# A delta layer's scan at five k-steps per chunk in every head pair, with later pairs begun sooner

## What is computed

```python
def gated_deltanet(h, w_in, conv_w, a_log, dt_bias, norm_w, w_out):
    proj = h @ w_in
    qkv = silu(causal_depthwise_conv(proj[..., :3 * DN_WIDTH], conv_w)); z = proj[..., 3 * DN_WIDTH:4 * DN_WIDTH]
    ...
    o = chunk_gated_delta_rule(q, k, v, beta, g)
    o = o * rsqrt(mean(o * o) + EPS) * norm_w * silu(z)
    return o @ w_out

def step(state, inp):            # the scan, one chunk after another
    q_c, k_c, u_c, w_c, a_c, gl = inp
    v_new = u_c - w_c @ state
    o_c = q_c @ state + a_c @ v_new
    state = state * gl + k_c.T @ v_new
    return state, o_c
```

## Time and profile before

| | |
|---|---|
| median of 3 runs | 1998.29 us (1997.29 to 1999.68) |
| the profiled execution's own time | 1997.75 us |
| its span | 1996.0 us |
| TensorE busy | 1964.0 us (98%) |
| VectorE busy | 1169.2 us (59%) |
| ScalarE busy | 845.9 us (42%) |

### The profile page before, as it was taken

How to read it: one execution, slowest core, us unless ns; L and a number is a source line. 1 busy time by engine, 2 the same in 40 slices (tenths; PEclk the granted TensorE clock), 3 DMA queues, 4 the chain that set the end, 5 groups by cost and what they waited for, 6 DMA issues and landing times.

```text
span 1996.0 us, 29508 instructions
## 1 busy us (share of the span) xinstructions
PE 1964.0 (98%) x11549; PEld 1616.6 (81%) x11549; DVE 1169.2 (59%) x1939; ACT 845.9 (42%) x1347; POOL 23.6 (1%) x28
## 2 busy tenths in 40 slices
PE   9999999999999999999999999999999899999998
PEld 7776798888888787898888888778778678888887
DVE  6556477534547766567533555877777656424532
ACT  5456544333335455454332333644664633212222
POOL 0111000000000000000000000000000000000000
PEclk9999999999999999999999999999999999999999
DMA  6222122222222111123223224111111122222221
GB/s 215 77 72 96 43 76 95 89 100 106 87 90 98 69 64 64 64 85 106 82 93 115 91 83 138 43 44 45 63 44 44 63 81 89 105 97 94 94 96 64
DMA packets 27583, 167.66 MB, mean 84 GB/s; under 512 B 3272, under 2 KB 3400, under 8 KB 11600
## 3 DMA queue, kind: packets, MB, share of 16 engines
q1 hardware_dynamic: 25872, 161.69, 23.0%
q10 hardware_dynamic: 1600, 4.42, 0.7%
HBM read 162.93 MB, written 2.11 MB: 83 GB/s over the span
## 4 chain that ended last, share of the span: by engine, by line
PE 85%; DVE 7%; ACT 5%; issue 2%; DMA 1%; SPq 0%; DVEq 0%; ACTq 0%
PE bank L506 24%; PE bank L508 24%; PE bank L507 23%; PE bank L1146 2%; PE bank L781 1%; ACT hH L1343 1%; ACT wH L1343 1%; DVE hL L2120 1%; PE bank L970 1%; PE bank L804 1%; PE bank L994 1%; DVE x L2116 1%; PE bank L793 1%; ACT L1343 1%; PE bank L1232 1%
## 5 line engine op out<-in xcount | busy, mean ns | idle before, releaser
L506 PE MATMUL bank<-hH,wH 128*128 128x512 f32 x1368 | 550.0, 402 | 2.0 <-DVE hL L2082 2.0
L508 PE MATMUL bank<-hH,wL 128*128 128x512 f32 x1368 | 532.9, 390 | 0.0
L507 PE MATMUL bank<-hL,wH 128*128 128x512 f32 x1368 | 531.9, 389 | 0.0
L1343 ACT ACTIVATE wH<-raw 128x2048 fp32r<-128x2048 f32 (+3 forms) x199 | 294.1, 1488 | 119.9 <-PE bank L508 105.1
L506 PEld LDWEIGHTS bank<-hH,wH 128*128 128x128 f32 x1368 | 257.4, 188 | 60.0 <-issue 7.1
L508 PEld LDWEIGHTS bank<-hH,wL 128*128 128x128 f32 x1368 | 257.2, 188 | 54.8
L507 PEld LDWEIGHTS bank<-hL,wH 128*128 128x128 f32 x1368 | 257.9, 189 | 46.4
L2031 DVE TENSOR_TENSOR wL<-raw,wH 128x2048 fp32r<-128x2048 f32 x96 | 219.7, 2288 | 125.6 <-ACT wH L1343 125.6
L506 PE MATMUL bank<-mH,wH 128*128 128x512 f32 (+1 forms) x610 | 232.8, 382 | 0.0
L507 PE MATMUL bank<-mL,wH 128*128 128x512 f32 (+1 forms) x610 | 232.6, 381 | 0.0
L508 PE MATMUL bank<-mH,wL 128*128 128x512 f32 (+1 forms) x610 | 232.6, 381 | 0.0
(11 more groups left out here) (344 smaller groups left out, 2864.4 us busy)
## 6 DMA issues: line engine op xcount, KB each, us to landing
raw<-in_ffn_up SPq DMA_DIRECT2D x44, 1024.0 KB, 4.8
raw<-in_mlp_up SPq DMA_DIRECT2D x16, 1024.0 KB, 4.8
raw<-in_mlp_down SPq DMA_DIRECT2D x16, 1024.0 KB, 4.8
raw<-in_ffn_down SPq DMA_DIRECT2D x16, 768.0 KB, 4.3
raw<-in_odd_in SPq DMA_DIRECT2D x12, 1024.0 KB, 4.8
raw<-in_dn_qkv SPq DMA_DIRECT2D x12, 1024.0 KB, 4.8
raw<-in_ffn_down SPq DMA_DIRECT2D x16, 640.0 KB, 3.8
raw<-in_even_in SPq DMA_DIRECT2D x7, 1024.0 KB, 4.9
```

What stands on the lines that cost most here:

```text
L506: mm(out, a, c, start=first, stop=False, skip_group_check=joined)
L507: mm(out, a, d, start=False, stop=False, skip_group_check=joined)
L508: return mm(out, b, c, start=False, stop=last, skip_group_check=joined)
L1343: return nc.scalar.activation(out, in_, func, **kw)
```

## The change

Before, pairs 0 to 2 take six steps per chunk and begin at steps 40, 88 and 136; pair 3 begins at 184, with five steps for each of its first four chunks and three steps for each of the rest, so its last write stands in step 215. After, all pairs take five, and begin at 40, 80, 124 and 172; the last write stands in step 211. The three points of a chunk stay two steps apart in all chunks of five or six steps (in those of three they were one step apart). The squares are taken at steps given by a list, and the roots of the last two pairs, and the scaling and turning back of pair 3, stand 1 to 20 steps sooner. Two lists of events that protect the buffer of squares are changed to fit.

```diff
         def scan_slot(p, n, f):
 
-            return 204 + 3 * (n - 4) + f if p == 3 and n >= 4 else 184 + 5 * n + (0, 2, 4)[f] if p == 3 else 48 * p + 40 + 2 * (3 * n + f)
+            return (40, 80, 124, 172)[p] + 5 * n + 2 * f
...
-        squared_at = [scan_slot(p, 4 * f + 3, 2) + (2 if (p, f) != (3, 1) else 1) for p in range(4) for f in range(2)]
-        scaled_at = [168, 172, 180, 184, 196, 200, 212, 219]
-        back_at = [170, 174, 182, 186, 198, 202, 214, 220]
-        roots = [(slice(0, 16), 143, 154, 155, (1, 1)), (slice(16, 24), 187, 190, 191, (2, 1)),
-                 (slice(24, 28), 207, 211, 212, (3, 0)), (slice(28, 32), 217, 218, 219, (3, 1))]
+        squared_at = [61, 81, 103, 121, 152, 165, 193, 212]
+        scaled_at = [168, 172, 180, 184, 196, 200, 211, 217]
+        back_at = [170, 174, 182, 186, 198, 202, 213, 218]
+        roots = [(slice(0, 16), 143, 154, 155, (1, 1)), (slice(16, 24), 167, 170, 171, (2, 1)),
+                 (slice(24, 28), 195, 205, 206, (3, 0)), (slice(28, 32), 214, 215, 216, (3, 1))]
...
-                act.wait_ge(*at(f"dn.os2.{f}" if p == 3 else f"dn.qsum{p + 1}" if f == 0 else f"dn.ksum{p + 2}" if p < 2 else "dn.qsum3"))
+                act.wait_ge(*at(f"dn.os2.{f}" if p == 3 else f"dn.qsum{p + 1}"))
...
-                        squares_of("k", p, 0, f"dn.qsum{p - 1}", *([f"dn.os{p - 2}.0"] if p >= 2 else []))
+                        squares_of("k", p, 0, f"dn.qsum{p - 1}", *([f"dn.os{p - 2}.0", f"dn.os{p - 2}.1"] if p >= 2 else []))
```

## The result

The changed kernel takes **2005.48 us** (median of 7, 2004.65 to 2007.29), the kernel before 1998.72 beside it (median of 7, 1997.29 to 1999.72): ratio 1.0034, with an interval of 1.0024 to 1.0043. It is slower by 6.8 us, on the side that was forecast and within the range, 3 us above the forecast. It is also above the 2000 to 2005 that the forecast had given itself. The profiled execution took 2005.62 us with a span of 2003.8 (before: 1997.75 and 1996.0); its mean granted clock is 0.996 for 0.998.

A forecast was written before the change was run, and what follows sets the result against it. The scan was taken as a chain round three engines, none full. Terms 4.2 + 0.4 + 2.6 + 1.5 + 1.0 - 1.7 - 0.6 - 3.7 = +3.7, plus 0.5 for longer matmuls, gave 2002.5 us, range 1995.5 to 2007.

The forecast's parts named there:

- Part 1: Pair 1, steps 96 to 100: state update behind VectorE's chain of five holds up the read of step 100; +4.2 us.
- Parts 2 to 4: Pairs 0 to 2: short write-to-read hand-over +2.6, late right sides at steps 75 and 124 +1.5, pair starts +1.0 and -1.7.
- the term of -1.7: Start of pair 2, begun at 124: table loads fall where ScalarE had been waiting; lost 1.3 for 3.0 us.
- the echo of part 1 in pair 2: Pair 2, step 146: the same VectorE chain falls ahead of the write of step 148; +0.4 us.
- the small waits that went: Pairs 0 to 2: small waits of the kernel before that disappear; -0.6 us.
- Part 5: Pair 3 and the outputs: losses of the three-step chunks go, new queueing comes; lost 6.7 for 10.4, -3.7 us.
- Nothing is late after it: After the last turning back: dn_out wants the result only at step 232, 9 us later, so nothing is lost or won.
- The clock: Rival, chance 0.16: clock falls after the 4.4 us wait in pair 1, one half-clock stretch costs 1.7 us; 2004.2.
- Table loads: Two more table loads on ScalarE (49 for 47), priced at 1.28 us each rather than 2.66 with the drain.
- Balance: Rival, chance 0.22: hand-overs and right sides are covered, 1.4 instead of 4.1 us; +1.5, 1999.8.
- VectorE on time: Rival, chance 0.14: VectorE reaches every state and right side in time except at pair 1's long wait; -5.5, 1992.8.
- pair 3 gives nothing: Rival, chance 0.08: pair 3's queues are as late in five steps as in three, gain 0; 2006.2 us.

The follow-up runs named there:

- the run with pair 0 alone: The kernel before with only pair 0 at five steps a chunk (its squares at steps 64 and 88): 2001.38 us, one time, beside 1999.79.

## Why the prediction was right, point by point

The waiting came out as forecast, +3.6 us in the table for +4.2 in the sum; what lies above it is 3.2 us of clock, which the sum had at nothing and one rival had once. That the waiting fits so well is in part luck, as the shares below show.

- *Part 1, the state behind the chain, +4.2.* Shown: the wait stands where it was said to (3.67), the state is 11.06 after the spread for 11.0, and without it steps 96 to 144 lose 4.1 less. Its cause was named rightly in two halves: the chain ahead of the state on VectorE, and vBlk with a table load ahead of the exponential on ScalarE. Mending either alone gives back 0.6 (chain) or 1.7 (exponential), without the clock; a place for the chunk where neither is in its way gives it all.
- *Parts 2 to 4, hand-over, right sides and the starts of pairs 1 and 2.* The sum of everything before pair 3 came out: +7.3 in the table for 4.2 + 0.4 + 2.6 + 1.5 + 1.0 - 1.7 - 0.6 = +7.4. The shares did not. Single waits had been read well: write of step 89 0.99 (1.3 in the working), solve of 92 0.97 (0.95), and the right sides of steps 75 and 124 0.59 and 0.91 (0.65 and 0.9). In the profile after, the reads of steps 75 and 95 stand at 1399.76 and 1425.28, those of 124 and 144 at 1478.76 and 1503.09. By the prediction's count either stretch needs 20.8 us (20 dense k-steps, four chunks, a sum, a small transpose). Without the right sides the start of pair 1 then loses 4.1, for 4.0 in the working, but that of pair 2 loses 2.6, for 1.3: the term of -1.7 is -0.4. With part 1 at 4.1 and the right sides at 1.5, only 1.0 is left for all other hand-overs, the echo of part 1 in pair 2 and the small waits that went, for which the working had 2.6 + 0.4 - 0.6 = 2.4. Pair 0 by itself agrees: 0.2 net by step 96. So the hand-overs were taken too dear and the start of pair 2 too cheap by about as much; that these cancel is luck. How the 1.0 divides was not measured.
- *Part 5, -3.7.* Measured -3.8, but half of it is from the roots of pair 2, whose two table loads no longer stand in pair 3, and only half from the new form of pair 3. The working counted all of it as pair 3 in five steps; following the queues gave the sum all the same. The waits: 0.55 at step 181 (0.55), 0.73 at 187 (1.15), 2.43 at the end (2.75). "Nothing is late after it" held, except for the clock.
- *The clock.* This is the term that was missing. It stood as a rival with 0.16 and 1.7 us, argued against by waits of up to 1.8 that had left the clock as it was in one profile. It came in addition to the forecast, and twice, behind 3.67 and behind 2.43, in both profiles of the changed kernel: 3.2 us of its 6.8. The working had the second wait too, at 2.75, and did not ask the same question of it. The page "TensorE: Matmul & The Clock Gate" of the Trainium skill (HAM oscillation) describes a kernel whose clock falls in each wait for a DMA, of some 3 to 5 us. The traces here agree for the wait of 3.67 (four of four profiles), and the clock fell behind the shorter ones of 2.4 as well (six of six); at 1.7 to 2.0 it fell in some and not in others.
- *Table loads.* Two more, at 1.28 each, with the next operation right behind (1431.47 and 1432.77): the 2.66 that the page "ScalarE: Activation LUTs" of the Trainium skill (What ACT_TABLE_LOAD costs) gives for a switch, load and drain together, was not seen, only the load.
- *Balance and VectorE on time* both had the long wait too. Their sums, 4.7 and 2.0 before pair 3, are excluded by the +7.3 there, though balance was near the truth on the hand-overs; *pair 3 gives nothing* is excluded by the -3.8.

## What to carry to other kernels

When a schedule is tightened, follow the queue of each engine at the one place where a chunk's update now falls behind a block of other work; a single such place cost more here than all the hand-overs that were shortened. Then give every wait of TensorE of some 2 us and more a second price, the clock behind it, and look first for a place where the waiting work has something to cover it, or for operations without haste that stand ahead of it. Moving one pair by three steps and the split of one weight half by three or four turned +6.8 us into -1.9, each against the kernel before beside it.

## What had not been expected of the hardware

A stretch at half clock of some 3.4 us cost 1.4 to 1.7 us in these comparisons, and 1.1 in one (pair 3 in the run with pair 0 alone). In the scan and at its end it followed each wait of 2.4 or 3.67 us (ten of ten), the wait of 1.8 ahead of one solve of pair 3 in two of four profiles (one of two of the kernel before), one of 1.93, and even one of 0.98 amid small matmuls, in both runs that have it; the waits of 1.72 and 2.01 were without it. Behind 1.67 it came only after a second wait, of 1.05, some 5 us later. Earlier, ahead of step 40, the wait of 2.38 for line 2649 was followed by it in the changed kernel's first profile and not in that of before. So the length of the wait alone does not decide it, and what else does stays open. In executions of one kernel the mean granted clock goes with it: 0.998 in most of the kernel before, 0.996 or 0.997 in all of the changed one, and 0.002 of 2000 us is 4 us, most of which two such stretches explain. Around that early wait the stretch was single, double or in two parts from one execution to the next, and the first read of the scan moved by up to 3.6 us with it.
